# A two-block transformer kernel: the first mixing output taken by row blocks, two norm vectors and a weight group loaded earlier, and the squares of the third hidden tile put ahead of the down weights

## The reference, cut to what matters

```python
# first block
h = _rms_norm(x, norm_mix_pre);  z = h @ w_in_first
attn = _rms_norm(_dilated_attention(q, k, v), attn_out_gain)      # 512 columns
rw = _rwkv7(...)    # a recurrence over the tokens, 512 columns; at its end:
#    out = (yn * gn_w + gn_b + bonus) * g
mixed = jnp.concatenate([attn, rw], axis=-1) @ w_out
x = x + _rms_norm(mixed, norm_mix_post)
h = _rms_norm(x, norm_ffn_pre)
f = jnp.square(jax.nn.relu(h @ w_ffn_up)) @ w_ffn_down            # 1024 -> 4096 -> 1024
x = x + _rms_norm(f, norm_ffn_post)
# second block
h = rms_norm(x, norm_mix_2);  proj = h @ w_in_2
x = x + jnp.concatenate([a, p], axis=-1) @ w_out_2                # attention, pooling
x = x + jnp.square(jax.nn.relu(rms_norm(x, norm_mlp_2) @ w_up_2)) @ w_down_2
return rms_norm(x, norm_final_2)
```

## Time and profile before

| | |
|---|---|
| median of 3 runs | 1308.94 us (1307.57 to 1309.18) |
| the profiled execution | 1306.41 us |
| its span, first to last instruction | 1304.7 us |
| PE busy | 1246.4 us, 96% of the span |
| DVE, ACT, POOL busy | 762.8, 583.1, 401.1 us |
| chain that ended last | PE 84%, DVE 7%, issue 4%, ACT 3% |
| mean granted TensorE clock | 0.994 of full speed |
| DMA | 109.40 MB, mean 84 GB/s |

### The profile page before, as it was taken

The page is one execution under the profiler, slowest core; times in us unless marked ns, Lnnn a source line. Parts: engine busy times, 40 slices in busy tenths (PEclk is TensorE's granted clock), DMA queues, the critical chain, the costliest instruction groups (busy, mean ns, idle before and its releaser), DMA issues.

```text
span 1304.7 us, 26571 instructions
## 1 busy us (share of the span) xinstructions
PE 1246.4 (96%) x11253; PEld 1145.2 (88%) x11253; DVE 762.8 (58%) x1027; ACT 583.1 (45%) x1026; POOL 401.1 (31%) x315
## 2 busy tenths in 40 slices
PE   7999989999789999999999999999999999999997
PEld 7677787888789899999999997776899999999997
DVE  5478735554448727639457467434475494673863
ACT  5445525445235525426246353445453262461642
POOL 7022226223002425235334224000051353343510
PEclk9999999999989999999999999999999999999999
DMA  6223300000152233323332423221223233333331
GB/s 209 65 65 97 97 2 3 3 3 5 64 194 66 98 97 98 101 71 121 99 96 89 139 74 97 66 65 44 84 83 102 76 115 102 94 101 94 98 114 65
DMA packets 102073, 109.40 MB, mean 84 GB/s; under 512 B 1970, under 2 KB 97252, under 8 KB 101956
## 3 DMA queue, kind: packets, MB, share of 16 engines
q1 hardware_dynamic: 101876, 107.45, 26.3%
q0 software_dynamic: 80, 0.26, 0.1%
HBM read 105.60 MB, written 2.10 MB: 83 GB/s over the span
## 4 chain that ended last, share of the span: by engine, by line
PE 84%; DVE 7%; issue 4%; ACT 3%; DVEq 1%; POOL 0%; DMA 0%; ACTq 0%; POOLq 0%
PE ps L528 10%; PE ps L529 10%; PE ps L530 10%; PE ps L619 6%; PE ps L620 6%; PE ps L621 6%; PE ps L493 4%; PE ps L495 4%; PE ps L494 4%; PE ps L579 1%; DVE w_lo L1787 1%; PE ps L581 1%; PE ps L580 1%; ACT w_hi L1200 1%; PE ps L804 1%
## 5 line engine op out<-in xcount | busy, mean ns | idle before, releaser
L528 PE MATMUL ps<-w_hi,a_hi 128*128 128x256 f32 x1024 | 287.0, 280 | 7.8 <-issue 7.8
L529 PE MATMUL ps<-w_lo,a_hi 128*128 128x256 f32 x1024 | 286.1, 279 | 0.0
L530 PE MATMUL ps<-w_hi,a_lo 128*128 128x256 f32 x1024 | 285.5, 279 | 0.0
L528 PEld LDWEIGHTS ps<-w_hi,a_hi 128*128 128x128 f32 x1024 | 192.4, 188 | 9.0 <-issue 8.9
L529 PEld LDWEIGHTS ps<-w_lo,a_hi 128*128 128x128 f32 x1024 | 192.5, 188 | 0.1
L530 PEld LDWEIGHTS ps<-w_hi,a_lo 128*128 128x128 f32 x1024 | 192.5, 188 | 0.0
L1787 DVE TENSOR_TENSOR w_lo<-w_raw,w_hi 128x2048 fp32r<-128x2048 f32 (+1 forms) x57 | 137.4, 2411 | 85.3 <-ACT w_hi L1200 85.0
L1200 ACT ACTIVATE w_hi<-w_raw 128x2048 fp32r<-128x2048 f32 (+1 forms) x57 | 108.2, 1899 | 133.2 <-PE ps L530 108.2
L2656 POOL TENSOR_TENSOR hsq<-tmp 128x512 f32<-128x512 f32 x64 | 91.2, 1441 | 102.8 <-ACT tmp L1312 75.1
L1893 DVE TENSOR_TENSOR w_lo<-w_raw,w_hi 128x1024 fp32r<-128x1024 f32 (+1 forms) x72 | 94.2, 1322 | 25.7 <-ACT w_hi L1273 25.5
L619 PE MATMUL ps<-th,w_hi 128*128 128x256 f32 x384 | 108.1, 281 | 0.8 <-ACT tmp L1298 0.8
(11 more groups left out here) (372 smaller groups left out, 3097.2 us busy)
## 6 DMA issues: line engine op xcount, KB each, us to landing
w_raw<-w_ffn_up_dram SPq DMA_DIRECT2D x16, 1024.0 KB, 5.7
w_raw<-w_ffn_down_dram SPq DMA_DIRECT2D x16, 1024.0 KB, 5.2
w_raw<-w_up_dram SPq DMA_DIRECT2D x16, 1024.0 KB, 5.7
w_raw<-w_down_dram SPq DMA_DIRECT2D x16, 1024.0 KB, 5.3
w_raw<-w_in_first_dram SPq DMA_DIRECT2D x12, 1024.0 KB, 5.3
w_raw<-w_out_dram SPq DMA_DIRECT2D x8, 1024.0 KB, 5.1
xn<-x_dram SPq DMA_DIRECT2D x8, 512.0 KB, 6.8
w_raw<-w_in_dram SPq DMA_DIRECT2D x4, 1024.0 KB, 5.5
```

What stands on the lines that cost most here:

```text
L528: mm(o, hi[:, hb + k, tok], whi, start=first and own and k == ks[0], stop=False, skip_group_check=True)
L529: mm(o, hi[:, hb + k, tok], wlo, start=False, stop=False, skip_group_check=True)
L530: m = mm(o, lo[:, hb + k, tok], whi, start=False, stop=last and k == ks[-1], skip_group_check=True)
```

## The change

It has two parts.

**The mixing output by row blocks.** The recurrence half of the input gets tiles of its own, `y_hi` and `y_lo`, which lie over memory that the attention has left. ACT and DVE split blocks 0 and 1 together, and block 2, right behind the last inverse (ahead of `carried` and of `received`); the last block is added by DVE in place of POOL, and split in two instructions on each engine. PE's second halves (`out_second`) wait by row block. SP waits for the last `solve` in place of the last `y_ready` for both norm vectors, then loads the last weight group, and loads only `x` behind the last `y_ready`.

**The squares ahead of the down weights.** In the stretch u = 3 of quarters 1 to 3 in both hidden layers (six places) ACT rectifies the tiles of u = 2 before it splits the first half of the down group and squares them before the second half; DVE takes their differences before the second half.

```diff
+            y_hi = r("y_hi", [P, HP, S], F32R)
+            y_lo = r("y_lo", [P, HP, S], F32R)
...
-            for c in range(1, 4):
+            for c in range(1, 3):
                 load(G_OUT1 + c, a["w_out"][0][:, cols_of(c)])
-                if c == 2:
-                    sp.wait_ge(sm["y_ready"], NB)
-                    load_gain(gpost, a["norm_mix_post"][0:1, :])
-                    for t in range(TT):
-                        load_x(t)
-                    load_gain(gpre, a["norm_ffn_pre"][0:1, :])
+            sp.wait_ge(sm["wu_done"], NB)
+            load_gain(gpost, a["norm_mix_post"][0:1, :])
+            load_gain(gpre, a["norm_ffn_pre"][0:1, :])
+            load(G_OUT1 + 3, a["w_out"][0][:, cols_of(3)])
+            sp.wait_ge(sm["y_ready"], NB)
+            for t in range(TT):
+                load_x(t)
...
+            def out_second(u):
+                g, b = G_OUT1 + u // 2, u % 2
+                for q in range(2):
+                    c = 2 * b + q
+                    for k in range(HP, KT):
+                        pe.wait_ge(sm["hlo_ready"], H_OUT1 + HP + (1, 1, 2, 3 + (k - HP) // 2)[c])
+                        m = row_product(ps[:, 4 + u, q * GW:(q + 1) * GW], rows(c), g, -HP, y_hi, y_lo, False, k == KT - 1,
+                                        ks=range(k, k + 1))
+                m.then_inc(sm["mm_done"], 1)
...
+            def upper_output(p, columns, blocks):
+                act.wait_ge(sm["y_ready"], blocks)
+                af(y_hi[:, p, columns], vy[:, p, columns], ACT.Copy).then_inc(sm["hhi_ready"], 1)
             solved(NB - 1, 2)
+            upper_output(slice(0, HP), slice(0, 2 * P), 2)
+            upper_output(slice(0, HP), rows(2), 3)
             carried(NB - 1, 0)
...
+            def lower_output(n, p, columns):
+                dve.wait_ge(sm["hhi_ready"], H_OUT1 + HP + n)
+                v.tensor_tensor(y_lo[:, p, columns], vy[:, p, columns], y_hi[:, p, columns].bitcast(F32), ALU.subtract)\
+                    .then_inc(sm["hlo_ready"], 1)
+            lower_output(1, slice(0, HP), slice(0, 2 * P))
+            lower_output(2, slice(0, HP), rows(2))
             received(NB - 1, 2)
...
+            v.tensor_tensor(vy[:, :, rows(3)], ysq[...], bonus[:, :, rows(3)], ALU.add).then_inc(sm["y_ready"], 1)
+            for p in range(2):
+                lower_output(3 + p, slice(2 * p, 2 * p + 2), rows(3))
...
-            shifted_output(NB - 1)
...
+                if u == 3:
+                    positive(b, q, 2, 0)
+                    positive(b, q, 2, 1)
+                    down_upper(group(b, q, 4), 0)
+                    copied(b, q, u, 1)
+                    square_high(2, 0)
+                    square_high(2, 1)
+                    down_upper(group(b, q, 4), 1)
+                    copied(b, q, u, 2)
+                    return
```

More of the change, by code:

```diff
@@ L188, in program @@
             rinv2 = r("rinv2", [P, 4 * H])
+        with ExitStack() as s:
+            r = held(s)
+            r("below_y", [P, HP * S])
+            y_hi = r("y_hi", [P, HP, S], F32R)
+            y_lo = r("y_lo", [P, HP, S], F32R)
         xs = xn[:, :, :].rearrange("q t (b s) -> q (t b) s", s=S)
@@ L677, in out_pair, with both @@
             def out_pair(n, g, tile):
-                last_pair(n, g, tile, lambda c, late: row_product(
-                    ps[:, (tile + c) % 4, late * GW:(late + 1) * GW], rows(c), g + late, 0, h_hi, h_lo, True, True))
+                def both(c, late):
+                    o = ps[:, (tile + c) % 4, late * GW:(late + 1) * GW]
+                    row_product(o, rows(c), g + late, 0, h_hi, h_lo, True, False, ks=range(HP))
+                    return row_product(o, rows(c), g + late, -HP, y_hi, y_lo, False, True, ks=range(HP, KT))
+                last_pair(n, g, tile, both)
             pe.wait_ge(sm["consts_built"], 1)
@@ L961, in out_part @@
                 pe.wait_ge(sm["o1_ready"], HP)
-                pe.wait_ge(sm["hlo_ready"], H_OUT1 + k1)
+                pe.wait_ge(sm["hlo_ready"], H_OUT1 + HP)
                 for q in range(2):
[L964 to L967, removed]
+                    row_product(ps[:, 4 + u, q * GW:(q + 1) * GW], rows(2 * b + q), g, 0, h_hi, h_lo, True, False,
+                                own=q == 0, ks=range(HP))
+            def out_second(u):
[7 more added lines that the diff above has]
+                m.then_inc(sm["mm_done"], 1)
             def beside(i, n):
@@ L1353, in up @@
                     upper_a22(b, q, u + 1)
[L1354 to L1357, removed]
+                upper_a(b, q, u + 1)
                 copied(b, q, u, 1)
[L1359 to L1362, removed]
+                upper_sum(b, q, u + 1, SUM2)
                 if u:
                     positive(b, q, u - 1, 0)
-                if u < 3:
-                    upper_sum(b, q, u + 1, SUM1)
+                upper_sum(b, q, u + 1, SUM1)
                 if u:
@@ L1655, in _ @@
             af(yrs[:, :], var[:, :], ACT.Sqrt).then_inc(sm["yrs_ready"], 1)
-            def second_half(src):
-                for p in range(HP):
-                    af(h_hi[:, HP + p, :], src[:, p, :], ACT.Copy).then_inc(sm["hhi_ready"], 1)
             def weights2(m):
@@ L1730, in in_and_attention @@
                         tick(32 + 8 * n + i)
-            act.wait_ge(sm["y_ready"], NB)
-            second_half(vy)
+            for p in range(2):
+                upper_output(slice(2 * p, 2 * p + 2), rows(3), NB)
             for u in range(4):
@@ L2321, in _ @@
             dve.drain()
+            v.tensor_tensor(vy[:, :, rows(3)], ysq[:, :, :].rearrange("q h n -> q (h n)").rearrange("q (p t) -> q p t", t=P),
+                            bonus[:, :, rows(3)], ALU.add).then_inc(sm["y_ready"], 1)
+            dve.drain()
+            for p in range(2):
+                lower_output(3 + p, slice(2 * p, 2 * p + 2), rows(3))
             def biased2(m):
@@ L2380, in window @@
                 dve.drain()
-            for p in range(HP):
-                lower(H_OUT1, HP + p, vy[:, p, :])
             dve.wait_ge(sm["gain_loaded"], 48)
```

50 lines of the change are left out of this document (24 added, 26 removed).

## The result

| | median us | lowest to highest | ratio to before, 95% interval |
|---|---|---|---|
| before | 1309.06 | 1307.57 to 1312.76 (4) | |
| changed | 1291.24 | 1287.83 to 1294.01 (4) | 0.9857 [0.9834, 0.988] |
| changed, profiled | 1293.62, span 1291.9 | clock 0.992 | |

The ratio times the 1308.94 us shown is 1290.2 us, where 1293.7 was forecast: the change gained 18.7 us in place of 15.3, and the value lies 0.6 us under the low end of the range. The profiled execution alone gained 12.8 us (1306.41 to 1293.62). So two things need an explanation: a gain larger than predicted, and a profile that shows less.

The account below looks back on a forecast made before the run. PE bounds the kernel, busy 1246.4 of 1304.7 us, so only its waits and low clock can be won. Savings of 7.47 us (mixing output) and 7.8 us (squares) took 1308.94 to 1293.7 us; range 1290.8 to 1299.5.

Parts of the forecast that it names:

- Ahead of the last block's end: Recurrence, before the last block ends: ACT's and DVE's new copies and differences fit into idle time, cost 0.
- Rival 4: Recurrence: ACT's new copies delay `Fb`, PE idles 3 us and its clock falls; slower, 1314.5 us; chance 4%.
- The last block and the clock: Mixing output: the 5.40 us wait goes whole and the clock stays up, 2.07 us more; 7.47 us together.
- The clock's bounds: Slow matmuls behind the mixing output's wait: gain between 0 and about 3.5 us, 2.07 taken.
- Transfers: Mixing output: norm vectors and last weight group load earlier, `x` stays hidden; PE had not waited for the vectors, so 0.
- what is late next: Mixing output: third weight group's split is just in time, 369.43 against 369.44; 0 taken, bounds 0 and 0.6 us.
- Part two: Hidden layers, six places: reordered squares remove PE's wait before the down group, 6 x 1.31 = 7.8 us, bounds 0 and 7.8.
- rival 1: Hidden layers: down weights become the bound, PE waits 1.0 us in place of 1.31; 1299.6 us; chance 8%.
- 2: Only one part pays, mixing output or squares, the other's gain being returned; 1301.3 us; chance 5%.
- 3: Hidden layer: late weight transfers take the saving back; no change, 1308.9 us; chance 3%.

Follow-up runs that it names:

- Experiment 4: Kernel before with 45 identity transposes keeping PE busy in the 5.4 us wait at the mixing output: 1309.16 us, ratio 0.9998.
- Experiment 5: Changed kernel with both norm vectors and the last output weight group again loaded behind the last block's addition: 1298.95 us, ratio 0.9911.
- experiment 10: Kernel before with transposes filling PE's waits in the recurrence and 45 more in its 5.4 us wait at the mixing output: 1307.98 us, ratio 0.997.
- experiment 7: Changed kernel with VectorE's order in the hidden layers as in the kernel before, ScalarE's still changed: 1294.04 us, ratio 0.9885.
- filled runs: Changed kernel with transposes into a bank nothing reads where PE waits in the recurrence, in two versions: medians 1290.17 and 1290.15 us.
- experiment 3: Kernel before with only the squares' order changed, mixing output as before: 1302.37 us, ratio 0.9944.
- experiments 6: Changed kernel with transposes into a bank nothing reads at PE's first two recurrence waits and in the last block's inverse: 1290.17 us, ratio 0.9848.
- experiment 9: Changed kernel with transposes filling PE's recurrence waits, including 14 behind the last block's key transposes: 1290.15 us, ratio 0.9837.

## Why the prediction was right or wrong

**The mechanism was right; two terms were too small, one of them with an upper bound that was wrong, and the range left out the clock's draws elsewhere.** The steps in turn:

- *Ahead of the last block's end*: hidden, as said. In the three traces of the changed kernel, and in that of the mixing part alone, the stretch of 350 to 355 us shifts by 0.00 us, and where no fall occurred the recurrence as a whole by 0.06. Rival 4 (slower, through the carry) did not come.
- *The last block and the clock*: 7.47 predicted, 7.81 or 7.82 measured in each of six traces that have this part. Experiment 4 shows the clock's part alone as 2.03 against 2.07, so the wait itself was worth 5.78 against the 5.40 of its row. The clock's bounds held, though the upper one was worked out wrongly: half again as many slow matmuls are 33 x 0.094 = 3.1 us, not 3.5.
- *Transfers*: the term 0 holds for the order as changed. But the prediction called the early loads hidden because PE had not waited for the vectors before. Experiment 5 shows what they are worth: 6.7 us. Before, that lateness lay in the shadow of the 5.4 us wait and of the slow matmuls behind it; without the slow ones alone, 1.3 us of it came out (experiment 10). The step "what is late next" had the right place (the third weight group, just in time, 0.2 us of room measured) and needs the loads to stay true.
- *Part two*: this is the step that failed by its size, "6 x 1.31 = 7.8 us, bounds 0 and 7.8": it measured 6 x 1.55 = 9.3, and the upper bound was wrong. The idle time in the row runs from the modelled end of a matmul, 0.28 us behind its start, while in an unbroken row the next one starts 0.12 us behind it. At the first stall the starts stood 1.586 us apart in place of 0.112, and the first matmul behind the wait took 0.195 in place of 0.118 to the next: 1.47 + 0.08 = 1.55. In experiment 7 a delay of 0.18 us between starts (0.295 for 0.112) did not make PE's list of waits at all, and cost 0.25. The order of events was as worked out: DVE's second weight half was ready 0.96 us ahead of PE (0.7 predicted), so rival 1 did not come, and neither did 2 or 3.
- *The sum and the range*: 7.81 + 9.3 = 17.1 against 15.3. The rest of 18.7 is the draw. 14 runs of the changed kernel and 40 of the kernel before can be sorted by their granted clock:

| | clock of the run | runs | mean us | lowest to highest |
|---|---|---|---|---|
| changed | 0.995 to 0.998 | 4 | 1288.7 | 1287.83 to 1289.55 |
| changed | 0.988 to 0.992 | 10 | 1293.7 | 1292.17 to 1294.88 |
| before | 0.992 to 0.997 | 12 | 1306.8 | 1305.45 to 1307.31 |
| before | 0.986 to 0.990 | 28 | 1311.4 | 1308.61 to 1314.66 |

(The runs of before in the first result are left out, since only the profiled one has its clock on record.) Like against like the change is worth 18.1 and 17.7 us; over all runs the means differ by 17.8, with a standard error of 0.75. The 4 runs of the first result held two of the changed kernel's four draws with the high clock, so their ratio came out on the large side, and the next measurement of the same kernel gave 0.9882 (1293.5 us), which would have been inside the range. The third gave 0.9854 (1289.8 us), outside again. 17.8 us would be 1291.1, just inside: the range had its low end too close, and which side the value fell on was chance. The prediction's "about 1 us of the runs (1307.57 to 1309.18)" took the scatter of three runs for that of the kernel; it is about 9 us from end to end (1305.45 to 1314.66).

That much of the scatter comes from falls in the recurrence is shown by the three traces of one program, and by the fillers: 10 filled runs of the changed kernel lie within 1289.17 to 1291.72 (standard deviation 0.8 us), 14 unfilled ones within 1287.83 to 1294.88 (2.4). For the kernel before it is carried over and not shown: its one trace is of the faster group, and none was taken of a run above 1310 us. The nearest is that of experiment 3, with a clock of 0.986, and it has both falls. The granted clock doesn't sort every kernel's runs either: in experiment 7 two runs with 0.994 and 0.995 took 1295.03 and 1294.56 us, longer than three with 0.991 and 0.992 (1292.87 to 1293.52).

What is not settled: why one draw falls and another does not, and whether the fillers themselves call up the fall at 350 us, which two of three filled traces show and none of the ten others. Nor why like against like gives 0.6 to 1 us more than the 17.1 of the traces. Part of the difference between single traces is small waits of PE for ACT's `tmp`, some 0.6 us each, which come at other places in each trace: the trace of before and the second of the changed kernel have one near 1232 us (in the time of the former) that the first and third lack, the second has one more near 1157 and the third near 690.

The Trainium skill, "TensorE: Matmul & The Clock Gate", section "Part 1: The HAM clock gate", was cited for the clock's monitor running freely, so that the count of slow matmuls differs from run to run. The traces agree, by the 20 and 16 slow distances behind the same wait (experiment 3), and go further: one program lost 0.06, 4.6 or 5.5 us in its recurrence. The prediction applied the rule only to the 2.07 us and not to the stretches that the change left alone. By the Trainium skill, "SBUF — State Buffer", section "Who interferes with whom", a DVE instruction with two SBUF inputs and a GpSimd one that reads SBUF exclude each other; the two instructions of L1959 took 1.62 us in the changed kernel, where they overlap POOL's squares (526.67 to 530.01), and 1.29 in experiment 7, where POOL had ended before they began. So the cost was there, and there was room for it.

## What to carry to other kernels

A stall is worth the distance between the starts of the two matmuls round it, less the usual distance, and a little for the slow first matmul: here 0.24 us more than the idle time shown, at each of the six stalls. When one wait goes, look at what was late in its shadow (here a norm vector's DMA) and move it in the same edit: the split by row blocks without the early loads gained 1.11 us of the 7.81 (the loads without the split were not run). And compare two traces matmul by matmul before a difference of totals is explained: two traces of one program differed by 4 us at places that nobody had touched.

## What the runs showed of the hardware that was not expected

The granted clock fell to half in the recurrence although PE's longest single wait there is 1.7 us; the waits in it are many and short. In the first trace of the changed kernel the first of two falls sets in at 186.9 us, right behind the first of two waits of 1.4 us, and lasts beyond the second. The trace without a fall looks the same up to there: from 183 to 187 us PE was busy for 1.88 us in both. This fall shows in six of the ten traces without fillers in the recurrence, of either kernel and the experiments, and the one at 334 us in eight of the ten; with the fillers neither shows in any of three (experiments 6, 9 and 10). One fall cost 2.5 to 2.7 us at 190 us and 1.9 to 3.1 at 334 to 344 us. The work that prevents it costs little but not nothing: with no fall in either, the 68 transposes of experiment 9 lengthened the recurrence by 0.9 us against the second trace of the changed kernel.

Waits of PE in the first trace of the changed kernel, 186 to 352 us:

```profile
PE ps L926 <- DVE negmax L2253: 2.5, 4, 0.7
PE ps L815 <- DVE hsq L2327: 1.8, 3, 0.9
PE ps L917 <- DVE rstd L2235: 1.7, 1, 1.7
PE ps L765 <- DVE LA L2190: 1.4, 1, 1.4
PE ps L773 <- DVE KA L2190: 1.4, 1, 1.4
```
